# Three layers on one core: feed-forward weights in the order of their use, and three instead of two weight units behind a norm

## The reference, cut to what matters

```python
shift, scale, gate = split(c @ mod_w[layer, 1] + mod_b[layer, 1], 3)
h = rms_norm(x, norm_w[layer, 1, 0]) * (1 + scale) + shift
y = swiglu(h, ffn_w_in[layer], ffn_w_out[layer])       # silu(h @ Wg) * (h @ Wu), then @ Wd
x = x + gate * rms_norm(y, norm_w[layer, 1, 1])
...
# third layer: a convolution over three rows on h @ Wg and h @ Wu first, no norm on y
```

## Time and profile before

| | us |
|---|---|
| median of 3 runs | 1039.26 (1035.68 to 1042.96) |
| profiled execution, device time | 1039.33 |
| its span | 1037.5 |
| PE busy | 975.5, 94% of the span |
| DVE busy | 801.6, 77% |
| ACT busy | 560.5, 54% |
| DMA moved | 228.65 MB, mean 220 GB/s |

### The profile page before, as it was taken

The page is one execution under the profiler, slowest core; times in us unless marked ns, Lnnn a source line. Parts: engine busy times, 40 slices in busy tenths (PEclk is TensorE's granted clock), DMA queues, the critical chain, the costliest instruction groups (busy, mean ns, idle before and its releaser), DMA issues. The chain is left out here.

```text
span 1037.5 us, 20177 instructions
## 1 busy us (share of the span) xinstructions
PE 975.5 (94%) x7912; PEld 940.9 (91%) x7912; DVE 801.6 (77%) x1434; ACT 560.5 (54%) x1130; POOL 4.6 (0%) x14
## 2 busy tenths in 40 slices
PE   4789988999999999998999999999989999999995
PEld 3788877999999999988999999999978989999995
DVE  2645898689888877887789888877777757877775
ACT  2234686544444456565455444446557457766663
POOL 0010000000000000000000000000000000000000
PEclk9688999999999999999999999999999999999998
DMA  9668577279987755850838877775622425554531
GB/s 339 285 167 263 177 277 284 86 282 356 340 308 300 283 216 196 312 180 2 299 119 312 314 301 299 304 263 220 211 94 81 143 82 185 203 182 183 183 139 41
DMA packets 63003, 228.65 MB, mean 220 GB/s; under 512 B 7090, under 2 KB 7346, under 8 KB 62804
## 3 DMA queue, kind: packets, MB, share of 16 engines
q1 hardware_dynamic: 62148, 225.07, 59.2%
q0 software_dynamic: 640, 2.10, 0.8%
q10 hardware_dynamic: 144, 0.52, 0.1%
HBM read 226.09 MB, written 1.57 MB: 219 GB/s over the span
## 5 line engine op out<-in xcount | busy, mean ns | idle before, releaser
L1895 PE MATMUL bank<-hH,wH 128*128 128x258 f32 (+1 forms) x1544 | 447.7, 290 | 17.4 <-DVE hL L1480 9.6
L1896 PE MATMUL bank<-hL,wH 128*128 128x258 f32 (+1 forms) x1544 | 440.7, 285 | 0.0
L1897 PE MATMUL bank<-hH,wL 128*128 128x258 f32 (+1 forms) x1544 | 438.9, 284 | 0.0
L1212 DVE TENSOR_TENSOR wL<-raw,wH 128x1024 fp32r<-128x1024 f32 x270 | 328.3, 1221 | 42.2 <-ACT wH L738 40.0
L1895 PEld LDWEIGHTS bank<-hH,wH 128*128 128x128 f32 x1544 | 295.2, 191 | 25.5 <-issue 9.1
L1896 PEld LDWEIGHTS bank<-hL,wH 128*128 128x128 f32 x1544 | 296.1, 192 | 0.4
L1897 PEld LDWEIGHTS bank<-hH,wL 128*128 128x128 f32 x1544 | 296.4, 192 | 0.0
L738 ACT ACTIVATE wH<-raw 128x1024 fp32r<-128x1024 f32 x270 | 276.5, 1048 | 35.8 <-PE bank L1897 21.0
L1895 PE MATMUL bank<-aH,wH 128*128 128x256 f32 x592 | 168.1, 284 | 5.0 <-DVE wL L1212 5.0
L1897 PE MATMUL bank<-aH,wL 128*128 128x256 f32 x592 | 167.5, 283 | 0.0
L1896 PE MATMUL bank<-aL,wH 128*128 128x256 f32 x592 | 167.5, 283 | 0.0
(11 more groups left out here) (329 smaller groups left out, 1026.5 us busy)
## 6 DMA issues: line engine op xcount, KB each, us to landing
raw<-in_weights SPq DMA_DIRECT2D x270, 512.0 KB, 4.6
modbuf<-in_mods SPq DMA_DIRECT2D x134, 512.0 KB, 6.2
strips<-bias_table POOLq DMA_DIRECT2D x8, 256.0 KB, 13.5
strips<-in_mods SPq DMA_DIRECT2D x3, 512.0 KB, 15.0
x<-in_xT SPq DMA_DIRECT2D x2, 512.0 KB, 6.3
crow<-in_c SPq DMA_DIRECT2D x2, 512.0 KB, 7.4
raw<-in_mods SPq DMA_DIRECT2D x2, 512.0 KB, 9.7
proj<-in_mods SPq DMA_DIRECT2D x2, 512.0 KB, 15.2
```

The costliest lines, as they stand in the source:

```text
L1212: V.tensor_tensor(wL[:, slot, :], raw[:, slot, :], wH[:, slot, :].bitcast(F32), ALU.subtract).then_inc(lo_ready[c], 1)
L1895: mm(out, lhs_h, rhs_h, start=start, stop=False, skip_group_check=True)
L1896: mm(out, lhs_h, rhs_l, start=False, stop=False, skip_group_check=True)
L1897: return mm(out, lhs_l, rhs_h, start=False, stop=stop, skip_group_check=True)
```

## The change

The units of a feed-forward stage are numbered in the order in which PE uses them: gate 0, up 0, gate 1, up 1, gate 2, up 2, down 0, gate 3, up 3, down 1, ..., gate 21, up 21, down 19, down 20, down 21. Before, the number was 3t, 3t + 1 and 3t + 2. The loads, the splits and the counts that they wait for are renumbered. In `step(t)` DVE and ACT now split the units from `next_units(t)` on: 3t + 4, 3t + 5 and 3t + 6 for t of 2 and more, where 3t + 6, 3t + 7 and 3t + 2 stood. Behind each norm but the one ahead of f2, PE multiplies three units instead of two as the rows of h come; f0's gate 1 gets bank 1.

```diff
+        def gate_unit(base, t):
+            return base + (2 * t if t < 2 else 3 * t - 2)
+        def down_unit(base, t):
+            return base + (3 * t + 6 if t < FT - 2 else 2 * FT + t)
+        def next_units(base, t):
+            return base + (2 * t + 6 if t < 2 else 3 * t + 4)
...
@@ SP, ffn
-                load_unit(base + 6)
-                load_unit(base + 7)
+                for p in range(6, 10):
+                    load_unit(base + p)
                 jobs_upto(Cursor.job + jobs_of(phase, 0))
+                for p in range(10, 12):
+                    load_unit(base + p)
                 for t in range(FT):
-                    load_unit(base + 3 * t + 9)
-                    load_unit(base + 3 * t + 10)
+                    p = next_units(base, t) + RING
+                    load_unit(p)
+                    load_unit(p + 1)
                     if t + 1 < FT:
                         jobs_upto(Cursor.job + jobs_of(phase, t + 1))
-                    load_unit(base + 3 * t + 8)
+                    if t >= 2:
+                        load_unit(p + 2)
...
@@ DVE, ffn, step
-                    nxt = base + 3 * t + 6
+                    nxt = next_units(base, t)
...
                         if t >= 2:
-                            split_low(base + 3 * t + 2)
-                    elif t == FT - 1:
-                        split_low(base + 3 * t + 2)
+                            split_low(nxt + 2)
...
@@ PE
-            def first_pair(p0, outs, a, width):
+            def first_units(p0, outs, a):
...
-                first_pair(base, gu_banks(phase, 0), a, HW)
+                first = dict(enumerate(gu_banks(phase, 0)))
+                if phase != "f2":
+                    first[2] = gu_banks(phase, 1)[0]
+                first_units(base, first, a)
                 gate_up(1)
...
-            first_pair(base, (bank[4], bank[5]), 4, HW)
-            for e in range(2, 8):
+            first_units(base, {n: proj_bank("sb", n) for n in range(3)}, 4)
+            turn_values("sb", 0)
+            for e in range(3, 8):
                 project("sb", e)
                 turn_values("sb", e - 2)
```

More of the change, by code:

```diff
@@ L474, in gu_banks @@
         def gu_banks(phase, t):
-            return (bank[0] if phase == "f0" and t == 0 else bank[4 + t % 2]), bank[7 - t % 2]
+            return (bank[t] if phase == "f0" and t < 2 else bank[4 + t % 2]), bank[7 - t % 2]
         def slot_of(a):
@@ L684, in _ @@
             ffn("f0")
-            for e in range(2, CD_UNITS):
+            for e in range(4, CD_UNITS):
                 load_unit(BASE["cd"] + e + RING)
@@ L688, in _ @@
             ffn("f1")
-            for e in range(2, SB_UNITS):
+            for e in range(4, SB_UNITS):
                 load_unit(BASE["sb"] + e + RING)
                 jobs_upto(JOBS_END["f1"] + min(KT, 2 * e // 3))
-                if e == 2:
+                if e == 4:
                     sp.dma_start(wst, A["w_s"]).then_inc(wst_landed, 16)
@@ L852, in at @@
                         return n if i is None else i * per + n
[L854 to L855 removed]
+                    nxt = next_units(base, t)
+                    up_class, up_count = cls(gate_unit(base, t) + 1)
                     act.wait_ge(unit_used[up_class], at(up_count, 2))
@@ L879, in step @@
                         last.then_inc(zc_ready, 1)
-                        if nxt < N_UNITS:
-                            split_high(nxt, i)
-                            split_high(nxt + 1, i)
+                        for p in (nxt, nxt + 1):
+                            if p < N_UNITS:
+                                split_high(p, i)
                         act.wait_ge(conv_ready, at(t + 1, 2))
@@ L886, in step @@
                     if t >= 2:
-                        down_class, down_count = cls(base + 3 * (t - 2) + 2)
+                        down_class, down_count = cls(down_unit(base, t - 2))
                         act.wait_ge(unit_used[down_class], at(down_count, 2))
@@ L892, in step @@
                         split_high(nxt + 1, i)
-                    if t >= 2:
-                        split_high(base + 3 * t + 2, i)
+                    if t >= 2 and nxt + 2 < N_UNITS:
+                        split_high(nxt + 2, i)
                 assert hi.at == base + RING
@@ L903, in ffn @@
                     step(t)
-                hi.at = base + 3 * FT + 5
+                hi.at = base + 3 * FT + 4
                 if phase != "f2":
                     shift_high(a)
-                    split_high(base + 3 * FT + 2)
+                    split_upto(base + 3 * FT + 5)
                 if phase == "f0":
@@ L1414, in step @@
                         V.tensor_tensor(sq[:, t % 2, S:2 * S], up_bank[:, 0:S], rstd[:, :], ALU.mult).then_inc(gu_scaled, 1)
-                        if t >= 2:
-                            split_low(base + 3 * t - 1)
+                        if t == 0:
+                            split_low(base + 5)
+                        if t >= 3 and nxt - 1 < N_UNITS:
+                            split_low(nxt - 1)
                         row = conv[:, t]
@@ L1439, in step @@
                                         ALU.mult).then_inc(af_ready, 1)
-                        if nxt < N_UNITS:
+                        if nxt + 1 < N_UNITS:
                             split_low(nxt + 1)
@@ L1448, in step @@
                         if t >= 2:
-                            split_low(base + 3 * t + 2)
-                    elif t == FT - 1:
-                        split_low(base + 3 * t + 2)
+                            split_low(nxt + 2)
                 for t in range(FT):
                     step(t)
-                lo.at = base + 3 * FT + 5
+                lo.at = base + 3 * FT + 4
                 if phase != "f2":
-                    split_low(base + 3 * FT + 2)
+                    split_upto(base + 3 * FT + 5)
             dve.wait_ge(par_landed, 16)
@@ L1934, in project @@
                 last.then_inc(unit_used[p % 3], 1)
-            def first_pair(p0, outs, a, width):
+            def first_units(p0, outs, a):
                 n = NORMS.index(f"A{a}")
-                slots = [(p0 + e) % RING for e in range(2)]
-                for e in range(2):
+                for e in outs:
                     unit_ready(p0 + e)
@@ L1943, in first_pair @@
                     pe.wait_ge(h_ready, KT * a + k + 1)
[L1944 to L1947, removed]
+                    cols = slice(k * P, (k + 1) * P)
+                    for e, out in outs.items():
+                        slot = (p0 + e) % RING
+                        last = three(out[:, 0:HW], wH[:, slot, cols], wL[:, slot, cols], hH[:, k], hL[:, k],
+                                     k == 0, k == KT - 1)
                         if k == KT - 1:
                             last.then_inc(unit_used[(p0 + e) % 3], 1)
-                    if a >= 1 and k in (3, 5):
+                    if k in (3, 5):
                         sum_square(n, (k - 3) // 2)
-                if a >= 1:
-                    sum_square(n, 2)
-                    sum_square(n, 3)
+                sum_square(n, 2)
+                sum_square(n, 3)
             def turn_values(phase, e):
@@ L2054, in gate_up @@
                     for n, bk in enumerate(gu_banks(phase, t)):
-                        p = base + 3 * t + n
+                        if (t, n) == (1, 0) and phase != "f2":
+                            continue
+                        p = gate_unit(base, t) + n
                         unit_ready(p, i)
@@ L2066, in down @@
                 def down(t, i=None):
-                    p = base + 3 * t + 2
+                    p = down_unit(base, t)
                     unit_ready(p, i)
@@ L2070, in down @@
                     slot = p % RING
+                    if phase == "f0" and t == 0:
+                        pe.wait_ge(gu_scaled, g0 + 2)
                     for m in range(KT):
@@ L2386, in _ @@
                 if e == 0:
-                    first_pair(base, (bank[4], bank[5]), 2, HW)
-                elif e >= 2:
+                    first_units(base, {n: proj_bank("cd", n) for n in range(3)}, 2)
+                elif e >= 3:
                     project("cd", e)
@@ L2641 @@
         for t in range(FT):
-            columns(BASE[name] + 3 * t, wi, t * P + r(P))
-            columns(BASE[name] + 3 * t + 1, wi, FF + t * P + r(P))
-            units[BASE[name] + 3 * t + 2] = wo[t * P:(t + 1) * P]
+            at = BASE[name] + (2 * t if t < 2 else 3 * t - 2)
+            columns(at, wi, t * P + r(P))
+            columns(at + 1, wi, FF + t * P + r(P))
+            units[BASE[name] + (3 * t + 6 if t < FT - 2 else 2 * FT + t)] = wo[t * P:(t + 1) * P]
     def tiles(v):
```

## The result

The change makes the kernel slower by 10%: 1142.3 us (median of 4 runs, 1138.3 to 1145.0) against 1039.75 us, ratio 1.0985, 95% interval 1.093 to 1.104. The forecast was 1085 us with a range to 1104. The direction and the place were right, the size was not. The profiled execution took 1145.0 us, with a span of 1143.2 us, 105.7 us more than the span before. Of the later kernels one execution of e5 (2385 us) and one of e6 (1080 us) were far slower than their others, and the ratios leave them out.

The account below looks back on a forecast made before the run. PE was taken to bound f0, f1 and f2, with the jobs' loads setting f0 and f1 after the change; 20.2 + 20.0 + 4.8 + 1.4 + 2.4 - 1.3 - 1.7 = +45.8 us on 1039.33 gave 1085 us, range 1064 to 1104.

Parts of the forecast that it names:

- The loop: f0 and f1: job, second split, one unit's issue, next job's landing take 9.3 us a step against 8.66; +20.2 and +20.0 us.
- Job to second split: DVE in a step of f1: 4.41 us from the first job's start to the second split's end.
- The landing: Job loads in f0 and f1: the job, second of two transfers on an idle queue, lands 4.86 us after the first's issue.
- The upper end of the range: Loop in f0 and f1: with landings on a backlogged queue, as one job 3.33 us late showed, some 10 us.
- Rival 2: Same loop with slower landings or half clock at the new waits: 9.8 us a step, 1105 us; chance 0.09.
- Half clock: PE matmuls might run at half clock after the new waits; part of the 1105 us rival, chance 0.09.
- Waits for jobs: DVE in f0 and f1: first jobs idle some 1.7 us for their DMA in nearly every step, 70 to 80 us in all.
- The tail: End of f0 and f1: from the last step's first job to the end of rstd, 11.8 and 10.9 us.
- The third unit: Behind norms of f0, cd, f1, sb: rstd 2.4 us later, costing 4.8 in f0 and f1 together, 1.4 in cd, 2.4 in sb.
- f2: Stage f2: PE's waits for low parts of weights shrink, -1.3 us at its start and -1.7 at its end.
- Rival 4: f0 and f1: jobs land in time, within 4.2 us after the second split; +2, 1041 us; chance 0.08.
- Rival 5: Whole kernel: PE's small waits go and later rstd costs nothing; -7, 1032 us; chance 0.04.

Follow-up runs that it names:

- e5: Changed kernel with next-step jobs issued ahead of all three units of a step, and two units behind each norm as before: 1036.98 us, ratio 0.9954.
- e6: Changed kernel with jobs ahead of all three units, and sb's first transposes moved behind the fourth unit: 1040.29 us, ratio 0.9998.
- e1: Changed kernel with the jobs of step t + 1 issued ahead of all three units of step t, nothing else: 1041.67 us, ratio 1.0019.
- e3: Kernel before, old unit order and two units behind a norm, with only the jobs moved behind the unit waiting for the third split: 1154.68 us, ratio 1.1101.
- e2: Changed kernel with the unit that waits for a step's first split moved behind the jobs: 1090.09 us, ratio 1.048.
- e4: Changed kernel with the jobs one place earlier, behind the first split's unit and ahead of the second's: 1041.63 us, ratio 1.0013.
- e7: Changed kernel with a step's two units exchanged, so both issue behind the second split and the job is third in one burst: 1148.89 us, ratio 1.1029.

## Why the prediction was wrong, by its own steps

- **The loop.** Right: where it is, what closes it, that DVE's 7.6 us of work do not set it, and that PE, SP and the tail follow from it. e1 and e3 show it from both sides.
- **Job to second split.** 4.41 forecast, 4.36 read in the step shown.
- **The landing. This step failed.** The prediction took 4.86 us on the ground that the queue "is idle when the pair is issued". It is not: the unit behind the first split went out 1.5 us ahead and lands 2.0 us later. The job is third, not second. 6.16 and 6.25 us instead of 4.86 are 1.3 and 1.4 us a loop, 27 and 29 us in the 21 loops of f0 and f1. The forecast was short by 1142.3 - 1085 = 57.3. From the first job of the stage to the last one 224.5 us (f0) and 225.3 us (f1) were measured, 196.2 forecast: 57.4 us together. e2, which moves just that unit behind the jobs, comes to 1090 us, 5 over the forecast. The unit's place stands in the rows of SP's stream with the change, and the price of a third transfer was to be had from the burst of the earlier trace rows: its third unit, issued at 601.44, took 5.3 us, so 0.85 + 5.3 = 6.15 from the first issue.

This is that landing, in the kernel before:

```profile
DMA to landing us min/median/max: 5.3/5.3/5.3
```

- **The upper end of the range.** "Some 10 us" a loop came from one late job. The mean was 10.6, so the bound cut off what it was to cover. Rival 2 had the direction, with 9.8.
- **Half clock**, the other half of rival 2, is not the cause. The granted clock was 0.94 over f0 and 0.95 over f1 against 1.00 before, but PE has no part in the loop: DVE starts each of the 21 first jobs of either stage when its own load lands.
- **The rule beside it.** The formula in the Trainium skill (DMA: Bandwidth & Descriptors, section Anatomy of one DMA — SWDGE (gpsimd) path) was fitted to DMAs issued by GpSimd and is 2.0 us plus the bytes at 436 GB/s; SP issues these here. It would have given 1068 for the pair, further off. Carried on to a third transfer it gives an estimate of 2.0 + 3 x 1.2 = 5.6 us from the first issue; the trace has 6.15, and the measurement decides.
- **Waits for jobs.** 70 to 80 us forecast in all, 72.4 + 74.3 = 146.7 measured in f0 and f1.
- **The tail.** From the last first job to the end of rstd 444.68 + 0.42 - 433.51 = 11.6 us in f0 and 823.31 + 0.42 - 812.43 = 11.3 in f1; forecast 11.8 and 10.9.
- **The third unit.** rstd 2.2 us later at each norm (2.4 forecast), cd +1.4 (+1.4), sb +2.7 (+2.4; 4.4 in e1, at a lower clock, which the prediction had named and left out of its sum). Right.
- **f2.** -2.9 (-3.0). Right.
- **Rival 4**, the jobs in time, priced at 1041 us, is what e1 (1041.67) and e4 (1041.63) gave once the jobs were. Its threshold, a landing 4.2 us after the second split, fits both sides, though nothing was run near it: 5.0 in e2 is over it, and costs 50 us; 3.5 to 3.7 in e4 is under it, and costs nothing.
- **Rival 5**, all small gains and no cost, was 1032 us. e5 shows what of it was real: the order without the third unit, -3 us by the medians and -5 by the ratio.

What stays open: why a unit issued 1.5 us ahead costs the job as much as one issued with it; why single landings of a job in the changed kernel reached 7.4 us and more; and why the clock of sb differs between kernels with the same code there.

## What to carry to other kernels

When entries of a queue are renumbered, write down for each the event that releases it and its step, before and after: a load that moves behind an entry released one step later has lost a whole step of its lead, even if it stands "at the same place" in the loop. If the release depends on what the load feeds, the loop's period is work plus issue plus landing, and it sets the pace as soon as it passes the bound engine's. Take the landing from the row with the same number of transfers issued ahead, those still in flight among them, not from an idle queue.

A load of small use (a job) ahead of loads with a step to spare costs the latter nothing: e1 has the same loads, and is 100 us faster.

## What the runs showed of the hardware

- Loads of 512 KB from one issuing engine land about in the order of their issue: alone 3.5 us, second 4.8 to 5.0, third 6.2 from the first issue of the burst. Loads issued behind one mostly do not delay it: in all nine traces (from 60 us on), a load issued less than 0.6 us behind one that found none of SP's loads in flight landed after 4.4 us (median of 26, 4.9 at most) with none issued behind it before it landed, and after 4.5 us (median of 249) with some. But 41 of those 249 took over 5.0 us, up to 6.9.
- A load issued 1.5 us ahead of the others delayed the job as much as one in the same burst did (10.57 and 10.70 us a step with it, 10.67 and 10.74 in e7). A forecast that credits the head start stays at the pair's 4.86 us, 1.3 to 1.4 us a step too low. The nine traces agree: behind one load that found none of SP's in flight, a load issued less than 0.6 us later lands after 4.4 us (median of 275), one issued 1.2 to 1.8 us later after 4.5 (103), one issued more than 1.8 us later after 3.9 (42), and one that finds none in flight after 3.5 (494).
- Behind PE's wait of 7.9 us at the end of f1 the matmuls stand 0.21 us apart for about 20 of them, then 0.12 again. Three of those rows, PE in time order with the change:

```profile
816.09 0.42 PE L1912 MATMUL bank<-aL,wH 128*128 128x256 f32 x1
816.30 0.42 PE L1913 MATMUL bank<-aH,wL 128*128 128x256 f32 x1
...
820.65 0.28 PE L1913 MATMUL bank<-aH,wL 128*128 128x256 f32 x1
```

The granted clock was 0.50 from 816 to 820 us, the lower of its two levels (1.2 GHz), as in the earlier trace rows. This stretch lay outside the loop that set the time.
